# A tile ring of 17 slots instead of 23, and a later place for the decay edges of a gated unit

## The reference, cut to what matters

```python
f = lbf + (1.0 - lbf) * sigmoid(f_logit); k = 1.0 - f; logf = log(f)
bc = cumsum(logf, within a chunk)
# per chunk
decay = exp(where(causal, bt[t] - bt[s], -inf))
a = einsum('bhtd,bhsd,bhtsd->bhts', qt, kt, decay)
o = einsum('bhts,bhsv->bhtv', a, vt) + einsum('bhtd,bhdv->bhtv', qt * exp(bt), state)
```

## Time and profile before

| | us |
|---|---|
| median of three runs | 2015.84 |
| lowest and highest of them | 2014.44, 2016.14 |
| the profiled execution | 2016.14 |
| its span, first to last instruction | 2014.4 |
| PE busy | 1963.2 |
| DVE busy | 991.8 |
| ACT busy | 759.6 |
| POOL busy | 280.4 |

### The profile page before, as it was taken

One profiled execution on the slowest core, in us unless ns is written; L12 is line 12 of the kernel. 1 busy time (PEld: TensorE's weight loads), 2 busy tenths in 40 slices (PEclk: granted clock), 3 DMA queues, 4 the chain that ended last, 5 costly groups with the idle time before them and its releaser, 6 DMA issues.

```text
span 2014.4 us, 22797 instructions
## 1 busy us (share of the span) xinstructions
PE 1963.2 (97%) x9064; PEld 1593.4 (79%) x9064; DVE 991.8 (49%) x1502; ACT 759.6 (38%) x1150; POOL 280.4 (14%) x273
## 2 busy tenths in 40 slices
PE   8989999989999999899999999999999999999997
PEld 6767788868888888688888878877887788888886
DVE  6676633474333334743343465765754454334334
ACT  5344522443223234432322355556543343223223
POOL 5121000231001011310100120221010011011012
PEclk9999999989999999899999999999999999999998
DMA  5212232423333323233333232211232233333321
GB/s 160 84 47 59 59 94 83 121 84 101 98 94 95 101 84 108 84 95 103 95 94 98 81 94 64 63 53 53 85 94 63 73 94 97 102 95 94 96 87 58
DMA packets 343403, 175.72 MB, mean 87 GB/s; under 512 B 6305, under 2 KB 343298, under 8 KB 343298
## 3 DMA queue, kind: packets, MB, share of 16 engines
q1 hardware_dynamic: 343298, 174.27, 29.8%
HBM read 172.15 MB, written 2.10 MB: 86 GB/s over the span
## 4 chain that ended last, share of the span: by engine, by line
PE 85%; DVE 8%; ACT 2%; issue 2%; POOL 2%; DMA 0%; SPq 0%; DVEq 0%; ACTq 0%; POOLq 0%
PE ps L962 26%; PE ps L966 26%; PE ps L964 26%; DVE WL L1371 1%; PE ps L1012 1%; PE ps L1029 1%; POOL TS L1732 1%; DVE TS L1404 1%; PE ps L1090 1%; POOL X L1758 1%; PE ps L1108 1%; PE ps L992 1%; PE ps L982 1%; PE ps L1021 1%; DVE TS L1569 1%
## 5 line engine op out<-in xcount | busy, mean ns | idle before, releaser
L1371 DVE TENSOR_TENSOR WL<-RAW,WH 128x1024 fp32r<-128x1024 f32 (+2 forms) x336 | 403.2, 1203 | 702.9 <-ACT WH L1147 702.6
L962 PE MATMUL ps<-HH,WH 128*128 128x512 f32 x1728 | 687.8, 398 | 6.6 <-DVE TS L1404 6.0
L966 PE MATMUL ps<-HL,WH 128*128 128x512 f32 x1728 | 679.8, 393 | 12.2 <-DVE HL L1381 12.0
L964 PE MATMUL ps<-HH,WL 128*128 128x512 f32 x1728 | 678.6, 393 | 3.8 <-DVE WL L1371 3.8
L1147 ACT ACTIVATE WH<-RAW 128x1024 fp32r<-128x1024 f32 (+2 forms) x336 | 342.2, 1021 | 541.9 <-PE ps L966 533.9
L966 PEld LDWEIGHTS ps<-HL,WH 128*128 128x128 f32 x1728 | 327.5, 190 | 87.6 <-DVE HL L1381 18.4
L962 PEld LDWEIGHTS ps<-HH,WH 128*128 128x128 f32 x1728 | 327.8, 190 | 81.5 <-DVE TS L1404 8.4
L964 PEld LDWEIGHTS ps<-HH,WL 128*128 128x128 f32 x1728 | 327.8, 190 | 74.3 <-DVE WL L1371 6.7
L962 PE MATMUL ps<-GH,WH 128*128 128x512 f32 x720 | 282.0, 392 | 0.0
L966 PE MATMUL ps<-GL,WH 128*128 128x512 f32 x720 | 280.6, 390 | 0.0
L964 PE MATMUL ps<-GH,WL 128*128 128x512 f32 x720 | 280.2, 389 | 0.0
(11 more groups left out here) (196 smaller groups left out, 1505.9 us busy)
## 6 DMA issues: line engine op xcount, KB each, us to landing
RAW<-in_ffn_w_gu SPq DMA_DIRECT2D x88, 512.0 KB, 3.8
RAW<-in_w_in SPq DMA_DIRECT2D x68, 512.0 KB, 3.9
RAW<-in_ffn_w_down SPq DMA_DIRECT2D x32, 512.0 KB, 4.1
RAW<-in_w_gate SPq DMA_DIRECT2D x22, 512.0 KB, 3.8
RAW<-in_w_up SPq DMA_DIRECT2D x22, 512.0 KB, 3.8
RAW<-in_w_out SPq DMA_DIRECT2D x16, 512.0 KB, 4.2
RAW<-in_mem_w_kv SPq DMA_DIRECT2D x16, 512.0 KB, 3.9
RAW<-in_w_down SPq DMA_DIRECT2D x16, 512.0 KB, 4.1
```

Of the source, the lines that this page charges most:

```text
L962: e.matmul(bk, wh, xh, start=k == 0, stop=False)
L964: e.matmul(bk, wl, xh, start=False, stop=False)
L966: last = e.matmul(bk, wh, xl, start=False, stop=k == kt - 1)
L1371: e.tensor_tensor(m["WL"][:, s, 0:kt, :], m["RAW"][:, n % NRAW, 0:kt, :], m["WH"][:, s, 0:kt, :].bitcast(F32), ALU.subtract).then_inc(*sg. ...
```

## The change

Three things are edited. The ring has 17 slots rather than 23. In gated_unit the second stage is left empty; prepare 2 to 6 come a stage later, each between two levels, and k_decay comes after level 5. The build leaves out the argument that set the scratch for dynamic DMAs to 4096 bytes a partition, so that it has the default of 16384.

```diff
-NTILE = 23
+NTILE = 17
@@ gated_unit
         self.prepare(u, 0, q, f)
         self.prepare(u, 1, q, f)
         yield
+        yield
+        self.level(u, 0)
         self.prepare(u, 2, q, f)
+        self.level(u, 1)
         self.prepare(u, 3, q, f)
         yield
-        self.level(u, 0)
-        self.level(u, 1)
+        self.level(u, 2)
         self.prepare(u, 4, q, f)
+        self.level(u, 3)
         self.prepare(u, 5, q, f)
         yield
-        self.level(u, 2)
-        self.level(u, 3)
+        self.level(u, 4)
         self.prepare(u, 6, q, f)
+        self.level(u, 5)
         self.tiles.take(("kd", u))
         self.step("k_decay", u, f)
-        yield
-        self.level(u, 4)
-        self.level(u, 5)
         yield
         self.level(u, 6)
@@ kernel
-    nc = _bacc.Bacc("TRN2", target_bir_lowering=False, num_devices=1, dynamic_dma_scratch_size=4096)
+    nc = _bacc.Bacc("TRN2", target_bir_lowering=False, num_devices=1)
```

## The result

The changed kernel takes 2029.05 us, median of four runs (2027.14 to 2029.81), against 2015.50 us of the kernel before beside it (2014.44 to 2016.14). The ratio is 1.0066, 95% interval 1.0049 to 1.0084: some 13.5 us slower. The forecast was 2020.5 with a range to 2023.5, so the direction was right and the time 8.5 us too low.

The account below looks back on a forecast made before the run. PE was taken to bound the kernel, so only new PE waits count. Three units at 1.6 us less 0.2 at L982 gave 4.6 us, 2020.7 from the profiled execution and 2020.4 from the median; forecast 2020.5, range 2016.2 to 2023.5.

Parts of the forecast that it names:

- PE is the bound and a new wait counts in full: Second block's mixer: PE busy 65.92 of 66 us in unit 1, so any new PE wait lengthens the run in full.
- Edges 2 and 3 in time with 1.2 us to spare: Units 1 to 3: edges ready near 1281.9 and 1283.2, before levels 2 and 3 need them; no cost.
- Edges 4 and 5, the chain step by step: Units 1 to 3: later preparation makes level 4 0.5 and level 5 1.1 us late, 1.6 us a unit.
- What the products cost: DVE's product pairs slowed by POOL's work: 1.3 us assumed for edge 4, 1.6 for edge 5.
- The rival in which the port is free: DVE's products not slowed by POOL, or half of them: +0 to +2.4 us, centre 2017; chance 0.31 with half free.
- GL beside edge 5's subtracts, 0.9 us: DVE's GL ahead of edge 4's products: 0.7 us alone, taken as 0.9 beside edge 5's subtracts on POOL.
- The scratch and the ring elsewhere at nothing: Larger scratch, and 17 tiles in the first block and SP's loads: waits are for events long past; cost 0.
- any shift before 1200 us: Sign that the forecast is wrong: a shift there would mean that the ring and not the order costs.
- The units' slack and R late: R late rival: WL or L1404 hold DVE as long as now, 3.3 us a unit, +9.9, 2026; chance 0.05.
- WL near 1268: Sign at unit 1's start: the forecast is wrong if WL on DVE at 1268 still takes 1.68 us.
- The 0.2 us given back at L982: Transposes' wait behind DVE, 0.8 us in all: PE comes 1.6 later, so 0.2 us is taken off the sum.
- The clock: Rival: each of three stalls brings 3.4 us at half clock, 1.7 us each, sum 2025.8; chance 0.03.

Follow-up runs that it names:

- the one wait on POOL: Changed kernel, with POOL starting edge 6 of units 1 to 3 only when DVE's products of edge 5 are done; 2018.79 us, ratio 1.0019.
- the second profile: The changed kernel run and profiled again with nothing altered; 2029.26 us, ratio 1.0073.
- The made stalls: Kernel before with 22 slots, PE made to wait for POOL memsets in the mixer or among large products; 2021.99 to 2034.43 us.
- the split stall of 0.43 + 1.01 us: Kernel before with 22 slots, PE made to wait for POOL memsets before levels 4 and 5 of units 1 to 3; 2030.6 us, ratio 1.0085.
- the unbroken 1.22 and 1.8: Kernel before with 22 slots, PE made to wait before level 4 of units 1 to 3 for two or three POOL memsets; 2022.75 and 2027.85 us.
- 2.4 us unbroken: Kernel before with 22 slots, PE made to wait before level 4 of units 1 to 3 for four POOL memsets; 2034.43 us, ratio 1.0093.
- three pauses of 0.71 us: Changed kernel's new order alone, with 23 slots and the 4096 scratch of the kernel before; 2019.0 us, ratio 1.0019.

## Why the prediction was wrong, point by point

- *PE is the bound and a new wait counts in full:* right for the idle time, 3.6 us of which delay the end by 5.0. But a wait was charged only once, and the larger part of its price came behind it (the last point).
- *Edges 2 and 3 in time with 1.2 us to spare:* right, with more to spare. POOL starts edge 2 at 1277.03, where 1278.5 was forecast; edge 3's second product ends at 1282.05, and levels 2 and 3 start at 1283.45 and 0.84 later, as before.
- *Edges 4 and 5, the chain step by step:* right to about 0.15 us. Forecast: R at 1287.3, edge 4 ready at 1291.3, edge 5 at 1293.25, levels late by 0.5 and 1.1. Measured: R at 1287.18, ready at 1291.19 and 1293.12, levels late by 0.5 and 1.1, 1.65 us a unit for a forecast of 1.6.
- *What the products cost:* right. The pairs took 1.26 and 1.68 us, for 1.3 and 1.6 assumed, and the one wait on POOL showed that it is the clash with POOL: without it 0.4 to 0.5 a product and no pause. The rival in which the port is free didn't happen. The argument against it was even stronger than I had it: POOL's run was 5.6 us (1287.26 to 1292.84), not 3.5.
- *GL beside edge 5's subtracts, 0.9 us:* it took 1.02. Edge 4's products then met edge 6's subtract (1290.12) and the last 0.2 us of edge 5's second one.
- *The scratch and the ring elsewhere at nothing:* right as far as the runs reach. The run with 19 slots and the larger scratch costs nothing, and with 17 the level 2 of unit 1, after 1283 us, starts within 0.2 us of where it did. The sign "any shift before 1200 us" was ill chosen: near 160 us the changed kernel is 2.3 us ahead, and at 200 us 0.8, because the clock fell at other moments in the first block, and kernels with other rings and other orders shift as much.
- *The units' slack and R late:* right that R is earlier than before, by 1.9 us, and that WL near 1268 is no longer slowed (1.22 us for 1.68).
- *The 0.2 us given back at L982:* right in kind, and small. The three waits of 0.3 us before L982 are gone in the changed kernel, and its transposes start 0.15 us earlier for it in the one unit whose clock did not fall (unit 2 of the second profile). From level 4 of that unit to that of the next it took 67.62 us, where before it was 66.07: 1.55 us. Three times that is 4.65, and the sum said 4.6; the sum without the clock was right to 0.1 us.
- *The clock:* this is the step that failed, a term that the sum put at nothing. I named the rival, but gave it 0.03, kept it out of the range and priced it at 1.7 us a stall. It happened, behind five of the six double pauses of the two profiles, at 3.1, 3.1 and 4.6 us in the first. I had taken one fall of the profile before, behind a stretch with half of its time idle, for the least that brings one about, and "0.5 and 1.1 us with work between" for an argument against it. The made stalls say the contrary: the eight small matmuls between the two pauses did not protect, for the clock fell behind the split stall of 0.43 + 1.01 us three times of three, behind the unbroken 1.22 and 1.8 once each, and only behind 2.4 us unbroken, which covers those matmuls with idle time, each time again. And the length was taken from the shortest fall (3.4 us); in rows 9 itself it is 6.8. At 6.8 us and half speed the loss is 3.4 a stall, and with all three the rival's sum would have been 4.6 + 10.2, or 2030.9, 2 us from what was measured.

The trace of before held more than I read from it. PE waited 1.77 us once, and the clock fell 0.8 us later, with 3.4 us at the lower level:

```profile
817.91 0.50 PE L966 MATMUL ps<-HL,WH 128*128 128x512 f32 x1 [1.77 <-DVE HL L1381]
```

```profile
818.70:822.10 3.40, 3.40 (x9) 2.63 (x8) 3.37 (x3) 1.25 (x2) 3.30 (x2) 0.50 0.02 5
```

A pause of 1.76 us, until 824.28, brought another fall, while pauses of 1.51 us (until 65.02), 1.59 (until 797.25) and even 2.59 (until 177.83) brought none. So falls behind pauses not much longer than the 1.6 us forecast for a unit could be seen beforehand, and so could their chance: 0.03 was too little for this rival, whatever the made stalls say.

## What to carry to other kernels

Where PE runs at 97 to 100% at the clock's higher level, price a new pause twice: once as idle time and once as what the clock may do behind it. In the mixer here single pauses up to 1.16 us brought no fall, and pauses that came to 1.2 us or more at one place, in the mixer or among the large products, brought one in 15 of 24 cases, for 1.6 to 4.9 us where it could be priced. Splitting a pause in two, with a few small matmuls between, did not make it safer. If a trace shows falls anywhere, a range for a change that adds pauses has to reach to one fall for each. And when DVE's operation before a bottleneck wait runs beside a POOL operation that nobody waits for soon, try one wait on POOL: here it gave back 10.5 of 14.5 us. Whether a trace was lucky is seen by setting the same matmuls of two traces against each other, stage by stage.

## What was not expected of the hardware

- The same kernel with the same pauses does not always get the same falls: three in one profile of the changed kernel, two in the next. Behind an unbroken pause of 1.8 us four runs went from 2024.14 to 2032.97 us.
- The loss does not grow with the idle time alone: three pauses of 0.71 us added 3.2 us to the kernel, three split ones of 1.44 added 15.9.
- In the changed kernel each slow stretch begins when the pause is over, 0.1 to 2.7 us behind it (pauses until 1293.18, 1364.03 and 1434.80, a clock of 0.50 from 1295.0, 1366.7 and 1434.9), and PE is fully busy in it, so the view of waits shows nothing of it. Only the clock column of the windows and the pitch of the matmuls do.
- The clash of DVE and POOL moves rather than goes: with k_decay early it fell on WL (2.06 us for 1.22), with POOL held back until R on the products (1.26 for 0.42), and with edge 6 held back on POOL itself (1.58 for 0.61), where it was free.
